# Six of adaLN's scale columns on TensorE from a second weight layout, and h's high part straight from PSUM

## The chip, the cores and the metric

One core of a Trainium2 chip runs the whole program in one launch. The time is the device time of one execution in microseconds (us); three executions of the kernel before were timed. Nothing below is averaged over cores, as there is one.

## What is computed

The reference is a decoder block on x of 512 tokens by 1024 channels, conditioned by one vector c of 1024 numbers. The change lies in its first lines:

```python
mod = jax.nn.silu(c) @ w_ada[l] + b_ada[l]
sh1, sc1, gt1, sh2, sc2, gt2 = jnp.split(mod[:, None, :], 6, axis=-1)
h = rmsnorm(x, norm_pre_mix[l]) * (1.0 + sc1) + sh1
y = token_mixer(h, w_in_mix[l], ...)
```

`mod` is a row of 6144 numbers, a product of one vector with a 1024 by 6144 matrix. The kernel keeps it as 48 columns of 128 (one number to a partition). The first 16 columns, `sh1` (8) and `sc1` (8), must be there before h is, and h is the input of every projection of the token mixer. Behind it stand a gated delta rule, the merge of two branches and an expert retrieval over 16384 rows, in which most of the time goes.

## The kernel before

The program is a row of stages that run one after the other; the change touches the first, `project_stage`. There, x (four tiles of 128 tokens) is squared and summed on ScalarE, scaled by 1/rms on VectorE (xn, L487), transposed in 128x128 blocks on TensorE into PSUM (`turn(k)`, L309; k counts eight blocks of 128 channels), and made into h (channels on partitions, 512 tokens) by one multiply and add with the columns `scale1` and `mod`. TensorE takes float32 products as three products of rounded parts, so every operand is split into a high part (float32r) and the rest: h into `h_hi` and `h_lo`, each weight tile into `w_hi` and `w_lo`.

What sets the order around the change is written out by hand, engine by engine, with semaphores:

- **SP** loads everything in one queue: c spread over partitions, four columns of adaLN's weights (each a 128x1024 tile, transposed, 512 KB, in a ring of eight slots `ada`), the four x tiles, twelve more columns, four projection tiles (`weight_ring`), then two columns and one tile by turns.
- **VectorE** makes each column of `mod` with one pass over a 128x1024 tile (`mod_column`, L475: multiply by silu(c) in PSUM, sum along the row). Per pair of channel blocks it takes four columns (two shifts, two scales) and then four tiny operations on 128x2 (L494, L495, L497, L499): add the bias to the shifts, to the scales, add 1, multiply by the norm's weight. Below, scale2, scale4 and scale6 are the ends of these for blocks 2 and 3, 4 and 5, 6 and 7. It also makes `h_lo` of the last two blocks (L503).
- **ScalarE** makes h twice per block: raw h from PSUM (L424), then its rounding `h_hi` (L427). After block 5 it rounds the first weight tile (`split(0)`, L416), after block 7 the second.
- **GpSimd** makes `h_lo` of blocks 0 to 5 (L385), and then the low part of each weight tile (`rest(n)`, L381).
- **TensorE** turns five blocks, then per block multiplies by the 40 columns of `w_ab` (three matmuls, L337, which end in the decay and beta gates), turns the next, and from block 6 on catches up with the first projection tile: 18 matmuls for blocks 0 to 5 (`project(0, q)`, L320), then blocks 6 and 7. Fifteen more tiles follow.

VectorE's work on the gates (from L507 on) waits for the last `w_ab` matmul, and the convolution of each projection tile (L520, L523) for the tile.

Of the kernel before, what the change touches and what calls it, by code (L numbers as in the profile page):

```python
# [226 lines left out]
def project_stage(nc, a, env):  # L227
# [11 lines left out]
    AR, K2 = 8, 2  # L239
    NB = 5  # L240
    ADA = [m for k in range(0, KT, K2) for m in (*range(SH1 + k, SH1 + k + K2), *range(SC1 + k, SC1 + k + K2))] + list(range(GT1, MOD))
    NA1 = 2 * KT
    N_HERE = N_QKV + N_Z
    with ExitStack() as ctx:
# [14 lines left out]
        dn_w = sb(ctx, "dn_w", [P, 12, 4])  # L259
        exp_a = sb(ctx, "exp_a", [H, 1])  # L260

        s_c, s_const, s_small, s_later, s_wab = (sem(ctx, n) for n in ("c_landed", "const_landed", "small_landed", "later_landed", "wab_landed"))
# [7 lines left out]
             "cols_turned", "gates_exped", "p_last"))  # L270
        V = Steps(sem(ctx, "p_vector"), ["eps"] + [f"{x}0" for x in ("shift", "scale_b", "scale_p", "scale")] + ["rstd"] + [f"xn{t}" for t in range(TT)]
                  + [f"{x}{k}" for k in range(K2, KT, K2) for x in ("shift", "scale_b", "scale_p", "scale")]
                  + ["a_bias", "a_max", "a_neg", "a_min", "b_plus", "beta", "softplus", "g", "G", "G_left", "cols", "be_g"])
        A = Steps(sem(ctx, "p_scalar"), ["c_silu"] + [f"sq{t}" for t in range(TT)] + ["std"] + [x for k in range(KT) for x in (f"h{k}", f"hi{k}")])
        E = Steps(sem(ctx, "p_tensor"), [f"xT{k}" for k in range(KT)])

        xT_ps, proj_ps, ss_ps, ab_ps = bank[0:NB], (bank[3], *bank[0:3]), bank[4], bank[5]
        spread_ps = (bank[5], bank[4])

        with nc.Block() as block:  # L280
            @block.sync
            def _(sp):
                def ada_load(n):
                    if n >= AR:
                        sp.wait_ge(ada_used, n - AR + 1)
                    sp.dma_start(ada[:, n % AR], a["w_ada"][ADA[n]]).then_inc(s_ada[n % AR], 16)

                sp.dma_start(c_in[:], a["c_row"]).then_inc(s_c, 16)
                for n in range(2 * K2):
# [3 lines left out]
                for n in range(2 * K2, NA1):  # L293
                    ada_load(n)
                for n in range(WRING):
# [80 lines left out]
            def _(pool):  # L376
# [6 lines left out]
                for k in range(KT - K2):  # L383
                    pool.wait_ge(*A.after(f"hi{k}"))
                    nc.gpsimd.tensor_tensor(h_lo[:, k, :], h_raw[:, k % 2], h_hi[:, k, :].bitcast(F32), ALU.subtract).then_inc(h_low, 1)  # L385
                for n in range(N_HERE + 2):
                    rest(n)

            @block.scalar
            def _(act):  # L390
                act.dma_start(w_ab[:], a["w_ab"]).then_inc(s_wab, 16)
                act.dma_start(g["cst"][:], a["wide"]).then_inc(s_const, 16)
# [75 lines left out]
            def _(dve):  # L468
# [8 lines left out]

                dve.wait_ge(*A.after("c_silu"))
                for k in range(0, KT, K2):
                    for n in range(2 * k, 2 * k + 2 * K2):  # L480
                        mod_column(n)
                        if n == 5:
                            dve.wait_ge(*A.after("std"))
                            nc.vector.reciprocal(stat[:, 2, :], stat[:, 1, :]).then_inc(*V.step("rstd"))
                            dve.wait_ge(*V.after("rstd"))
                            for t in range(TT):
                                nc.vector.tensor_scalar(xn[:, t * D:(t + 1) * D], x_tok[:, t, :], stat[:, 2, t:t + 1], None, ALU.mult).then_inc(*V.step(f"xn{t}"))  # L487
                    if k == 0:
                        dve.wait_ge(s_small, 16 * 3)
                    if k == K2:  # L490
                        dve.wait_ge(s_later, 16 * 6)
                    dve.wait_ge(ada_used, 2 * k + 2 * K2)
                    sh, sc = slice(SH1 + k, SH1 + k + K2), slice(SC1 + k, SC1 + k + K2)
                    nc.vector.tensor_tensor(mod[:, sh], mod[:, sh], b_ada[:, sh], ALU.add).then_inc(*V.step(f"shift{k}"))  # L494
                    nc.vector.tensor_tensor(mod[:, sc], mod[:, sc], b_ada[:, sc], ALU.add).then_inc(*V.step(f"scale_b{k}"))  # L495
# [35 lines left out]
                for n in range(N_QKV):  # L531
# [25 lines left out]
                assert n_ada + 8 == MOD  # L557
                for m in range(8):
# [7 lines left out]
                dve.wait_ge(ada_used, MOD)  # L566
                nc.vector.tensor_tensor(mod[:, GT1:MOD], mod[:, GT1:MOD], b_ada[:, GT1:MOD], ALU.add).then_inc(last_v, 1)
# [1582 lines left out]
def lay_out(inputs):  # L2150
# [3 lines left out]
    def cols(w, c0, n):  # L2154
# [58 lines left out]
```

## Time and profile before

| | us |
|---|---|
| median of three runs | 1857.72 (1857.22 to 1857.79) |
| profiled execution, first to last instruction | 1856.8 |
| TensorE busy | 1768.2 (95%) |
| VectorE busy | 1307.3 (70%) |
| ScalarE busy | 742.8 (40%) |
| GpSimd busy | 764.5 (41%) |

The span of the profiled execution is 0.9 us under the median of the runs, which hold what lies before the first and after the last instruction too; no separate time of the profiled execution is given. In 40 slices of 46 us each, TensorE is at 0.8 or more of a slice everywhere but in the first (0.3) and one in the middle (0.7), and VectorE at 0.5, 0.9, 0.9 and 0.3 in the first four. The DMA engines are at 0.9 in the first slice and 0.0 to 0.6 in the next ten. TensorE's granted clock is 0.981 of full speed over the span.

### The profile page before, as it was taken

Reading aid. Unit: us, or ns where it says so; the run is one execution under the profiler, and the core shown is the slowest. Engines: PE = TensorE matmul, PEld = TensorE weight load, DVE = VectorE, ACT = ScalarE, POOL = GpSimd, SP = SyncE. Lnnn points to the kernel's source line nnn. Section 1 sums busy time; section 2 is a strip of 40 time slices with the busy share of each in tenths; the row PEclk is TensorE's granted clock in tenths of the full one; section 3 lists DMA queues with packets and bytes.
Section 4 is the critical chain, followed back from the end, with each engine's and each line's share of the span. In section 5 each row is a group of like instructions: output and inputs, shape, how many; then the busy total and the mean of one; then the engine's idle time right before and its main releaser. Section 6 shows DMA issues by size and latency. Waiting matters only on the chain. (4 is left out here: it accounts for less than half of the span.)

```text
span 1856.8 us, 31058 instructions
## 1 busy us (share of the span) xinstructions
PE 1768.2 (95%) x11485; PEld 1564.7 (84%) x11485; DVE 1307.3 (70%) x2777; ACT 742.8 (40%) x1227; POOL 764.5 (41%) x449
## 2 busy tenths in 40 slices
PE   3999999999998989999999999879999999999998
PEld 2666888878877889999999999879998888888887
DVE  5993454553224679878869999756787888777777
ACT  4332332242234233333337767633333333333334
POOL 2333232344442448777753333122454443332330
PEclk9998999999999999999999999989999999999999
DMA  9661101022322249888868999978899999889883
GB/s 356 217 233 71 36 16 34 25 91 91 102 79 103 91 141 314 282 292 292 286 235 281 341 311 331 319 264 285 287 317 337 370 370 359 326 320 328 316 325 145
DMA packets 179267, 432.64 MB, mean 233 GB/s; under 512 B 15816, under 2 KB 91720, under 8 KB 179040
## 3 DMA queue, kind: packets, MB, share of 16 engines
q1 hardware_dynamic: 125088, 273.71, 42.5%
q0 software_dynamic: 36864, 134.23, 20.3%
q10 hardware_dynamic: 17216, 23.36, 3.4%
q8 instruction: 63, 1.03, 0.2%
q14 instruction: 36, 0.29, 0.0%
HBM read 383.54 MB, written 47.71 MB: 232 GB/s over the span
## 5 line engine op out<-in xcount | busy, mean ns | idle before, releaser
L201 POOL DMA_INDIRECT own_rows<-in_peer_v_dram,own_row x128 | 212.3, 1659 | 330.8 <-DVE y_own L2094 312.7
L1988 PE MATMUL banks<-v_hi,coef_lo 128*128 128x512 f32 x756 | 294.6, 390 | 0.0
L1988 PE MATMUL banks<-v_lo,coef_hi 128*128 128x512 f32 x756 | 294.5, 390 | 0.0
L1988 PE MATMUL banks<-v_hi,coef_hi 128*128 128x512 f32 x756 | 294.1, 389 | 0.1
L201 POOL DMA_INDIRECT own_rows<-in_u_rows_dram,own_row x128 | 160.6, 1255 | 233.1 <-DVE own_rows L1733 178.8
L2079 DVE TENSOR_TENSOR v_lo<-weight_ring,v_hi 128x1024 fp32r<-128x1024 f32 x128 | 156.5, 1222 | 24.7 <-ACT v_hi L2027 22.7
L1988 PEld LDWEIGHTS banks<-v_hi,coef_hi 128*128 128x128 f32 x756 | 142.0, 188 | 29.5 <-issue 0.5
L1988 PEld LDWEIGHTS banks<-v_hi,coef_lo 128*128 128x128 f32 x756 | 141.9, 188 | 29.5
L1988 PEld LDWEIGHTS banks<-v_lo,coef_hi 128*128 128x128 f32 x756 | 141.9, 188 | 28.9
L2094 DVE SCALAR_TENSOR_TENSOR y_own<-own_rows,own_coef,y_own 128x1024 f32<-128x1024 f32 x128 | 163.8, 1279 | 1.9 <-DVE y_own L2094 0.5
L1397 PE MATMUL banks<-h_hi,wring_hi 128*128 128x384 f32 (+2 forms) x448 | 155.2, 347 | 4.0 <-ACT gelu_early L1479 2.9
L2027 ACT ACTIVATE v_hi<-weight_ring 128x1024 fp32r<-128x1024 f32 x128 | 135.1, 1055 | 59.4 <-PE banks L1988 48.1
L1527 POOL TENSOR_TENSOR wring_lo<-weight_ring,wring_hi 128x1024 fp32r<-128x1024 f32 x54 | 129.6, 2399 | 65.4 <-ACT wring_hi L1469 65.3
L1397 PE MATMUL banks<-h_lo,wring_hi 128*128 128x384 f32 (+2 forms) x448 | 154.0, 344 | 0.0
L1397 PE MATMUL banks<-h_hi,wring_lo 128*128 128x384 f32 (+2 forms) x448 | 153.9, 344 | 0.0
L2031 ACT ACTIVATE coef_hi<-coef 128x384 fp32r<-128x384 f32 x128 | 67.0, 524 | 211.6 <-DVE coef L2117 211.6
L1469 ACT ACTIVATE wring_hi<-weight_ring 128x1024 fp32r<-128x1024 f32 x54 | 57.3, 1061 | 158.4 <-PE banks L1397 157.9
L1665 DVE SCALAR_TENSOR_TENSOR own_rows<-own_rows,banks 128x1024 f32<-128x1024 f32 x64 | 77.8, 1215 | 52.3 <-DMA own_rows<-in_u_rows_dram,own_row 52.3
L2079 DVE TENSOR_TENSOR coef_lo<-coef,coef_hi 128x384 fp32r<-128x384 f32 x128 | 71.3, 557 | 57.5 <-ACT coef_hi L2031 57.5
L2117 DVE TENSOR_TENSOR coef<-gelu,gate_tiles 128x384 f32<-128x384 f32 x128 | 70.8, 553 | 45.8 <-ACT gelu L2041 45.8
L1165 POOL TENSOR_TENSOR wring_lo<-weight_ring,wring_hi 128x1024 fp32r<-128x1024 f32 x26 | 64.1, 2465 | 88.7 <-ACT wring_hi L1185 88.7
L1787 PE MATMUL banks<-query_hot 128*128 128x128 f32 x768 | 93.6, 278 | 6.7 <-ACT gate_block L1834 5.0
(393 smaller groups left out, 4346.1 us busy)
## 6 DMA issues: line engine op xcount, KB each, us to landing
weight_ring<-in_peer_v_dram SPq DMA_DIRECT2D x128, 512.0 KB, 5.4
weight_ring<-in_peer_u_dram SPq DMA_DIRECT2D x68, 512.0 KB, 4.5
ada<-in_w_ada_dram SPq DMA_DIRECT2D x48, 512.0 KB, 5.7
gate_scratch<-gate_block SPq DMA_DIRECT2D x48, 512.0 KB, 7.0
gate_tiles<-gate_scratch SPq DMA_DIRECT2D x32, 768.0 KB, 6.9
gelu_scratch<-gelu_early ACTq DMA_DIRECT2D x104, 192.0 KB
gelu<-gelu_scratch SPq DMA_DIRECT2D x104, 192.0 KB, 5.6
u_early<-in_peer_u_dram SPq DMA_DIRECT2D x36, 512.0 KB, 7.1
```

Of the source, the lines that this page charges most:

```text
L201: pool.indirect_dma_start(own_rows[:, n % R], None, tables[n // NS], bass.IndirectOffsetOnAxis(ap=own_row[:, n % NS:n % NS + 1], axis=0)). ...
L1165: nc.gpsimd.tensor_tensor(w_lo[:, b % 2], wring[:, b], w_hi[:, b % 2].bitcast(F32), ALU.subtract).then_inc(lo_ready, 1)
L1397: last = nc.tensor.matmul(out, ww[n % HR][:, k, :], x[:, k, t0:nt], start=(k == 0 and m == 0), stop=(k == KT - 1 and m == 2))
L1527: nc.gpsimd.tensor_tensor(w_lo[n % HR][:], w[:, n % WR], w_hi[n % HR][:].bitcast(F32), ALU.subtract).then_inc(lo_ready, 1)
L1665: nc.vector.scalar_tensor_tensor(rows[:, i % R], rows[:, i % R], 1.0, h_psum[:], ALU.mult, ALU.mult, accum_out=own_act[:, bass.ds(n, 1)]). ...
L1787: last = nc.tensor.matmul(bank[2 * (u % 2) + t // 4][:, t % 4 * P:(t % 4 + 1) * P], hot1[:, u % RH, t, :], hot2[:, u % RH, t, :], start=Tr ...
L1988: last = nc.tensor.matmul(y_bank(t, half)[:], w[:, j, t * P:(t + 1) * P], x[:, j, c], start=(first and n == 0), stop=False)
L2027: nc.scalar.activation(v_hi[:, e % G], vt[:, e % G], ACT.Copy).then_inc(v_hi_ready, 1)
L2031: nc.scalar.activation(c_hi[:, e % G], coef[:, e % 2], ACT.Copy).then_inc(c_hi_ready, 1)
L2079: return nc.vector.tensor_tensor(dst, src, hi.bitcast(F32), ALU.subtract)
L2094: nc.vector.scalar_tensor_tensor(y_own[:], rows[:, n % R], own_coef[:, n - NS:n - NS + 1], y_own[:], ALU.mult, ALU.add).then_inc(row_used, 1)
L2117: nc.vector.tensor_tensor(by_block(coef[:, p % 2]), by_block(gel[:, j]), gt[:, i % 2, :, j, :], ALU.mult).then_inc(coef_ready, 1)
```

## The change

- A second layout of the weights, `w_ada_k`, holds the scale columns of blocks 2 to 7 with the contraction on the partitions (512 KB each, as before, now in `qkvT`'s space, which is free until the first convolution). TensorE makes each with eight float32 matmuls of 128x128 weights and one moving column, silu(c) as a column (`c_col`, 128x8, a new small load and a new activation), into bank 3.
- VectorE makes 10 columns ahead of the projections in place of 16; the scale's bias is added straight from PSUM (L520 in the new file).
- ScalarE makes `h_hi` from PSUM in one pass. VectorE makes raw h from PSUM (`raw(k)`, three buffers `h_raw`), for `h_lo` alone.
- Four blocks are turned ahead in place of five, since bank 3 is taken; the first projection tile, whose bank is 3 too, waits for the last use of it (`scale_b6`).
- `split(0)` moves up behind block 3 on ScalarE, and `rest(0)` on GpSimd behind block 3's `h_lo`.

```diff
-    NB = 5
-    ADA = [m for k in range(0, KT, K2) for m in (*range(SH1 + k, SH1 + k + K2), *range(SC1 + k, SC1 + k + K2))] + list(range(GT1, MOD))
-    NA1 = 2 * KT
+    NB = 4
+    ADA = [SH1, SH1 + 1, SC1, SC1 + 1] + list(range(SH1 + K2, SH1 + KT)) + list(range(GT1, MOD))
+    NA1 = KT + K2
...
+                for q in range(0, NPE, K2):
+                    for n in range(2 * K2 + q, 2 * K2 + q + K2):
+                        ada_load(n)
+                    for n in range(q, q + K2):
+                        sp.dma_start(ada_k[:, n], a["w_ada_k"][n]).then_inc(s_adak[n], 16)
+                    if q == K2:
+                        sp.dma_start(wring[:, 0], a["w_proj"][0]).then_inc(s_w[0], 16)
...
+                def ada_columns(q0):
+                    for q in range(q0, q0 + K2):
+                        pe.wait_ge(s_adak[q], 16)
+                        for k in range(KT):
+                            last = nc.tensor.matmul(ada_ps[:, q:q + 1], ada_k[:, q, k, :], c_col[:, k:k + 1], start=(k == 0), stop=(k == KT - 1))
+                        last.then_inc(ada_col, 1)
+
+                pe.wait_ge(c_col_ready, 1)
+                ada_columns(0)
                 pe.wait_ge(s_const, 16)
                 pe.wait_ge(*V.after(f"xn{TT - 1}"))
                 for k in range(NB):
                     turn(k)
+                pe.wait_ge(*V.after("scale_b2"))
+                ada_columns(K2)
...
+                            pe.wait_ge(*V.after("scale_b6"))
                             pe.wait_ge(lo_ready, 1)
...
                     if k + NB < KT:
+                        pe.wait_ge(*A.after(f"hi{k}"))
+                        pe.wait_ge(*V.after(f"raw{k}"))
                         turn(k + NB)
+                    if k == 1:
+                        pe.wait_ge(*V.after("scale_b4"))
+                        ada_columns(2 * K2)
...
-                    nc.scalar.activation(h_raw[:, k % 2], xT_ps[k % NB][:], ACT.Identity, bias=mod[:, SH1 + k:SH1 + k + 1],
-                                         scale=scale1[:, k:k + 1]).then_inc(*A.step(f"h{k}"))
-                    act.wait_ge(*A.after(f"h{k}"))
-                    nc.scalar.activation(h_hi[:, k, :], h_raw[:, k % 2], ACT.Copy).then_inc(*A.step(f"hi{k}"))
-                    if k == KT - 3:
+                    nc.scalar.activation(h_hi[:, k, :], xT_ps[k % NB][:], ACT.Identity, bias=mod[:, SH1 + k:SH1 + k + 1],
+                                         scale=scale1[:, k:k + 1]).then_inc(*A.step(f"hi{k}"))
+                    if k == 3:
                         split(0)
...
+                    src = ada_ps[:, k - K2:k] if by_pe else mod[:, sc]
+                    nc.vector.tensor_tensor(mod[:, sc], src, b_ada[:, sc], ALU.add).then_inc(*V.step(f"scale_b{k}"))
...
+                def raw(k):
+
+                    dve.wait_ge(*A.after(f"hi{k}"))
...
+                    if HRAW <= k < KT - K2 + HRAW:
+                        dve.wait_ge(h_low, k - HRAW + 1)
+                    nc.vector.tensor_scalar(h_raw[:, k % HRAW], xT_ps[k % NB][:], scale1[:, k:k + 1], mod[:, SH1 + k:SH1 + k + 1],
+                                            ALU.mult, ALU.add).then_inc(*V.step(f"raw{k}"))
```

On SP, the loads behind the x tiles (`w_ada` is the old layout, `w_ada_k` the new). Before:

```order
L292 DMA x_tok<-in_x_dram 128x1024 x4
L286 DMA ada<-in_w_ada_dram 128x1024 x4
L286 DMA ada<-in_w_ada_dram 128x1024 [waits ada_used] x8
L296 DMA weight_ring<-in_w_proj_dram 128x1024 x4
L286 DMA ada<-in_w_ada_dram 128x1024 [waits ada_used] x2
```

Now:

```order
L301 DMA x_tok<-in_x_dram 128x1024 x4
L295 DMA ada<-in_w_ada_dram 128x1024 x2
L306 DMA qkvT<-in_w_ada_k_dram 128x1024 x2
L295 DMA ada<-in_w_ada_dram 128x1024 x2
L306 DMA qkvT<-in_w_ada_k_dram 128x1024 x2
L308 DMA weight_ring<-in_w_proj_dram 128x1024
L295 DMA ada<-in_w_ada_dram 128x1024 [waits ada_used] x2
L306 DMA qkvT<-in_w_ada_k_dram 128x1024 x2
L310 DMA weight_ring<-in_w_proj_dram 128x1024 x3
```

The same 16 loads stand in another order, with the first projection tile (L308) five places ahead of the last pair of columns.

On TensorE, the start of the program. Before:

```order
L309 MATMUL banks<-cst,xn 128x128 [waits p_vector,const_landed]
L309 MATMUL banks<-cst,xn 128x128 x19
L337 MATMUL banks<-h_hi,wab_parts 40x512 [waits h_low_ready,ab_lo_ready]
L337 MATMUL banks<-h_lo,wab_parts 40x512
L337 MATMUL banks<-h_hi,wab_parts 40x512
L309 MATMUL banks<-cst,xn 128x128 x4
```

Now (the pair L330 on `ada_k_landed4` and `5` comes behind two more blocks, in the same form):

```order
L330 MATMUL banks<-c_col,qkvT 128x1 [waits ada_k_landed0,c_col_silu]
L330 MATMUL banks<-c_col,qkvT 128x1 x7
L330 MATMUL banks<-c_col,qkvT 128x1 [waits ada_k_landed1]
L330 MATMUL banks<-c_col,qkvT 128x1 x7
L323 MATMUL banks<-cst,xn 128x128 [waits p_vector,const_landed]
L323 MATMUL banks<-cst,xn 128x128 x15
L330 MATMUL banks<-c_col,qkvT 128x1 [waits ada_k_landed2,p_vector]
L330 MATMUL banks<-c_col,qkvT 128x1 x7
L330 MATMUL banks<-c_col,qkvT 128x1 [waits ada_k_landed3]
L330 MATMUL banks<-c_col,qkvT 128x1 x7
L363 MATMUL banks<-h_hi,wab_parts 40x512 [waits h_low_ready,ab_lo_ready]
```

Forty-eight matmuls on one column stand in the queue ahead of, between and behind the turns.

On VectorE, from the end of xn to block 3. Before (L494 to L499 are the four tiny operations):

```order
L475 SCALAR_TENSOR_TENSOR ada,mod<-ada,banks 128x1024 [waits ada_landed6]
L475 SCALAR_TENSOR_TENSOR ada,mod<-ada,banks 128x1024 [waits ada_landed7]
L494 TENSOR_TENSOR mod<-mod,b_ada 128x2 [waits ada_used,later_landed]
L495 TENSOR_TENSOR mod<-mod,b_ada 128x2
L497 TENSOR_SCALAR scale<-mod 128x2 [waits p_vector]
L499 TENSOR_TENSOR scale<-scale,norms 128x2 [waits p_vector]
L475 SCALAR_TENSOR_TENSOR ada,mod<-ada,banks 128x1024 [waits ada_landed0]
```

Now (four lines of the tiny operations for blocks 2 and 3 come first, then):

```order
L508 SCALAR_TENSOR_TENSOR ada,mod<-ada,banks 128x1024 [waits ada_landed6]
L508 SCALAR_TENSOR_TENSOR ada,mod<-ada,banks 128x1024 [waits ada_landed7]
L533 TENSOR_SCALAR h_raw<-banks,scale,mod 128x512 [waits p_vector,p_scalar]
L533 TENSOR_SCALAR h_raw<-banks,scale,mod 128x512 [waits p_scalar]
L516 TENSOR_TENSOR mod<-mod,b_ada 128x2 [waits ada_used]
L520 TENSOR_TENSOR mod<-banks,b_ada 128x2 [waits ada_column_done]
L522 TENSOR_SCALAR scale<-mod 128x2 [waits p_vector]
L524 TENSOR_TENSOR scale<-scale,norms 128x2 [waits p_vector]
L533 TENSOR_SCALAR h_raw<-banks,scale,mod 128x512 [waits p_vector,p_scalar]
L533 TENSOR_SCALAR h_raw<-banks,scale,mod 128x512 [waits h_low_ready,p_scalar]
```

The tiny operations of a pair now wait for TensorE (`ada_column_done`), and the passes that make raw h stand between the column passes in VectorE's queue.

## Rows read from the trace of the kernel before

**Rows 1.** The page's first line.
```profile
span 1856.8 us, 31058 instructions
```
**Rows 2.** Stretches of 5 us: length, busy us (instructions) by engine, PEclk, DMA share, GB/s.
```profile
core 0: us, PE busy (x) PEld busy (x) DVE busy (x) ACT busy (x) POOL busy (x), PEclk, DMA share, GB/s
...
35.00:40.00 5.00, 2.71 (x6) 0.66 (x6) 4.97 (x9) 2.89 (x5) 4.20 (x3) 0.74 1.03 410
40.00:45.00 5.00, 4.26 (x12) 3.37 (x12) 2.56 (x7) 3.66 (x5) 0.69 (x1) 0.57 0.78 257
45.00:50.00 5.00, 5.00 (x23) 3.67 (x22) 0.00 (x0) 1.12 (x2) 2.39 (x1) 1.00 0.57 176
50.00:55.00 5.00, 5.00 (x23) 4.11 (x23) 4.84 (x6) 3.13 (x5) 2.39 (x1) 1.00 0.86 325
```
**Rows 3.** Timeline, 22 to 41 us: start, duration, engine, line, operation.
```profile
22.54 2.74 DVE L487 TENSOR_SCALAR xn<-x_tok,stat 128x1024 f32<-128x1024 f32 x4
...
25.42 4.50 PE L309 MATMUL banks<-cst,xn 128*128 128x128 f32 x20 [25.42 <-DVE xn L487]
...
30.84 0.60 PE L309 MATMUL banks<-cst,xn 128*128 128x128 f32 x4
...
31.08 2.63 POOL L385 TENSOR_TENSOR h_lo<-scT,h_hi 128x512 fp32r<-128x512 f32 x2 [0.34 <-ACT h_hi L427]
...
32.89 0.84 DVE L494 TENSOR_TENSOR mod<-mod,b_ada 128x2 f32<-128x2 f32 x1
...
34.03 0.16 DVE L499 TENSOR_TENSOR scale<-scale,norms 128x2 f32<-128x2 f32 x1
...
38.33 2.35 POOL L381 TENSOR_TENSOR wring_lo<-weight_ring,wring_hi 128x1024 fp32r<-128x1024 f32 x1
...
38.79 1.91 DVE L494 TENSOR_TENSOR mod<-mod,b_ada 128x2 f32<-128x2 f32 x1
...
40.74 0.80 PE L320 MATMUL banks<-h_hi,wring_hi 128*128 128x512 f32 x1 [0.81 <-POOL wring_lo L381]
```
**Rows 4.** Timeline: the matmul behind the first 18 of tile 0, and VectorE's next work.
```profile
47.27 0.40 PE L337 MATMUL banks<-h_hi,wab_parts 128*40 128x512 f32 x1
...
50.06 0.74 DVE L507 TENSOR_SCALAR xn<-banks,dt_bias 8x512 f32<-8x512 f32 x1 [5.29 <-PE banks L337]
```
**Rows 5.** Single loads: the fifth column, the first projection tile; issue and landing.
```profile
L286 SPq DMA_DIRECT2D ada<-in_w_ada_dram x1: 443/443/443, 5.8 to 5.8; - x1
...
DMA to landing us min/median/max: 14.1/14.1/14.1
...
L296 SPq DMA_DIRECT2D weight_ring<-in_w_proj_dram x1: 432/432/432, 28.0 to 28.0; - x1
...
DMA to landing us min/median/max: 7.3/7.3/7.3
```
**Rows 6.** Groups by line, 0 to 165 us: passes from PSUM to SBUF.
```profile
L520 DVE TENSOR_SCALAR xn<-banks,dn_w 128x512 f32<-128x512 f32 x12 | 8.7, 728 | 2.7 <-PE banks L320 2.7
...
L424 ACT ACTIVATE scT<-banks,mod,scale 128x512 f32<-128x512 f32 x8 | 6.2, 770 | 10.6 <-PE banks L309 5.2 <-DVE scale L499 5.1 <-POOL h_lo L385 0.2
```
**Rows 7.** Small matmuls: weight loads with eight moving columns; float32 matmuls of a line.
```profile
L370 PEld LDWEIGHTS banks<-cst,decay_rows x12: 133/137/138, 93.9 to 94.6; 8*128 8x128 f32 x12
...
L364 PE MATMUL banks<-scT,cst 128*16 128x512 f32 x16 | 8.9, 637 | 4.3 <-ACT scT L440 4.3
```
**Rows 8.** Timeline, the delta stage: VectorE between two GpSimd operations.
```profile
186.06 0.76 POOL L736 TENSOR_TENSOR AT<-LT,cst 128x256 f32<-128x256 f32 x1
186.19 1.17 DVE L924 SCALAR_TENSOR_TENSOR qgT<-qkv_tile,egT 128x512 f32<-128x512 f32 x1
186.76 1.20 POOL L737 TENSOR_TENSOR CT<-LT,cst 128x256 f32<-128x256 f32 x1
```
**Rows 9.** Stretches of 0.2 us of line L771 (matmuls of 8 rows): PE, PEld, PEclk.
```profile
172.40:172.60 0.20, 0.20 (x4) 0.20 (x4) 1.00 0.00 0
...
173.40:173.60 0.20, 0.20 (x4) 0.20 (x4) 1.00 0.00 0
...
174.00:174.20 0.20, 0.00 (x0) 0.00 (x0) 0.50 0.00 0
```

More of the change, by code:

```diff
@@ L260, in project_stage @@
         exp_a = sb(ctx, "exp_a", [H, 1])
+        c_col = sb(ctx, "c_col", [P, KT])
+        ada_k = qkvT[:].rearrange("p (q n) t -> p q (n t)", q=NPE).rearrange("p q (k m) -> p q k m", k=KT)
+        ada_ps = bank[3]
+        s_ck, c_col_ready, ada_col = sem(ctx, "c_col_landed"), sem(ctx, "c_col_silu"), sem(ctx, "ada_column_done")
+        s_adak = [sem(ctx, f"ada_k_landed{q}") for q in range(NPE)]
         s_c, s_const, s_small, s_later, s_wab = (sem(ctx, n) for n in ("c_landed", "const_landed", "small_landed", "later_landed", "wab_landed"))
@@ L292, in _ @@
                     sp.dma_start(x_tok[:, t, :], a["x"][t * P:(t + 1) * P, :]).then_inc(s_x[t], 16)
-                for n in range(2 * K2, NA1):
-                    ada_load(n)
-                for n in range(WRING):
+                for q in range(0, NPE, K2):
[5 more added lines that the diff above has]
+                        sp.dma_start(wring[:, 0], a["w_proj"][0]).then_inc(s_w[0], 16)
+                for n in range(1, WRING):
                     sp.dma_start(wring[:, n], a["w_proj"][n]).then_inc(s_w[n], 16)
@@ L384, in _ @@
                     pool.wait_ge(*A.after(f"hi{k}"))
-                    nc.gpsimd.tensor_tensor(h_lo[:, k, :], h_raw[:, k % 2], h_hi[:, k, :].bitcast(F32), ALU.subtract).then_inc(h_low, 1)
-                for n in range(N_HERE + 2):
+                    pool.wait_ge(*V.after(f"raw{k}"))
+                    nc.gpsimd.tensor_tensor(h_lo[:, k, :], h_raw[:, k % HRAW], h_hi[:, k, :].bitcast(F32), ALU.subtract).then_inc(h_low, 1)
+                    if k == 3:
+                        rest(0)
+                for n in range(1, N_HERE + 2):
                     rest(n)
@@ L390, in _ @@
             def _(act):
+                act.dma_start(c_col[:], a["c_col"]).then_inc(s_ck, 16)
                 act.dma_start(w_ab[:], a["w_ab"]).then_inc(s_wab, 16)
@@ L401, in _ @@
                 last.then_inc(*A.step("c_silu"))
+                act.wait_ge(s_ck, 16)
+                nc.scalar.activation(c_col[:], c_col[:], ACT.Silu).then_inc(c_col_ready, 1)
                 for dst, name in small[3:]:
@@ L476, in mod_column, with scales @@
                                                    accum_out=mod[:, m:m + 1]).then_inc(ada_used, 1)
[L478 to L492, printed above, removed]
+                def scales(k):
                     sh, sc = slice(SH1 + k, SH1 + k + K2), slice(SC1 + k, SC1 + k + K2)
+                    by_pe = k >= K2
+                    dve.wait_ge(ada_used, 2 * K2 + k if by_pe else 2 * K2)
                     nc.vector.tensor_tensor(mod[:, sh], mod[:, sh], b_ada[:, sh], ALU.add).then_inc(*V.step(f"shift{k}"))
-                    nc.vector.tensor_tensor(mod[:, sc], mod[:, sc], b_ada[:, sc], ALU.add).then_inc(*V.step(f"scale_b{k}"))
+                    if by_pe:
+                        dve.wait_ge(ada_col, k)
+                    src = ada_ps[:, k - K2:k] if by_pe else mod[:, sc]
+                    nc.vector.tensor_tensor(mod[:, sc], src, b_ada[:, sc], ALU.add).then_inc(*V.step(f"scale_b{k}"))
                     dve.wait_ge(*V.after(f"scale_b{k}"))
@@ L499, in _ @@
                     nc.vector.tensor_tensor(scale1[:, k:k + K2], scale1[:, k:k + K2], norms[:, 0, k:k + K2], ALU.mult).then_inc(*V.step(f"scale{k}"))
+                def raw(k):
+                    dve.wait_ge(*A.after(f"hi{k}"))
+                    if k % K2 == 0:
+                        dve.wait_ge(*V.after(f"scale{k}"))
+                    if HRAW <= k < KT - K2 + HRAW:
+                        dve.wait_ge(h_low, k - HRAW + 1)
+                    nc.vector.tensor_scalar(h_raw[:, k % HRAW], xT_ps[k % NB][:], scale1[:, k:k + 1], mod[:, SH1 + k:SH1 + k + 1],
+                                            ALU.mult, ALU.add).then_inc(*V.step(f"raw{k}"))
@@ new lines, in low @@
+                def low(k):
+                    dve.wait_ge(*A.after(f"hi{k}"))
+                    dve.wait_ge(*V.after(f"raw{k}"))
+                    nc.vector.tensor_tensor(h_lo[:, k, :], h_raw[:, k % HRAW], h_hi[:, k, :].bitcast(F32), ALU.subtract).then_inc(h_low_end, 1)
+                dve.wait_ge(*A.after("c_silu"))
+                for n in range(2 * K2):
+                    mod_column(n)
+                dve.wait_ge(s_small, 16 * 3)
+                scales(0)
+                for n in range(2 * K2, 3 * K2):
+                    mod_column(n)
@@ new lines, in _ @@
+                dve.wait_ge(*A.after("std"))
+                nc.vector.reciprocal(stat[:, 2, :], stat[:, 1, :]).then_inc(*V.step("rstd"))
+                dve.wait_ge(*V.after("rstd"))
+                for t in range(TT):
+                    nc.vector.tensor_scalar(xn[:, t * D:(t + 1) * D], x_tok[:, t, :], stat[:, 2, t:t + 1], None, ALU.mult).then_inc(*V.step(f"xn{t}"))
+                dve.wait_ge(s_later, 16 * 6)
+                scales(2)
+                for n in range(3 * K2, 4 * K2):
+                    mod_column(n)
@@ L501, in _ @@
+                raw(0)
+                raw(1)
+                scales(4)
+                raw(2)
+                raw(3)
+                for n in range(4 * K2, NA1):
+                    mod_column(n)
+                raw(4)
+                raw(5)
+                scales(6)
                 for k in range(KT - K2, KT):
-                    dve.wait_ge(*A.after(f"hi{k}"))
-                    nc.vector.tensor_tensor(h_lo[:, k, :], h_raw[:, k % 2], h_hi[:, k, :].bitcast(F32), ALU.subtract).then_inc(h_low_end, 1)
+                    raw(k)
@@ L504, in _ @@
+                for k in range(KT - K2, KT):
+                    low(k)
                 nc.vector.tensor_scalar(neg_sel[:], sel_head[:, :, 0:1].rearrange("h n o -> h (n o)"), -1.0, None, ALU.mult)
@@ L2171, in lay_out @@
         "c_row": np.broadcast_to(f["c"], (P, D)),
+        "c_col": f["c"][0].reshape(KT, P).T,
+        "w_ada_k": cols(f["w_ada"][0], (SC1 + 2) * P, KT - 2),
         "w_ada": f["w_ada"][0].T.reshape(MOD, P, D),
```

21 lines of the change are left out of this document (12 added, 9 removed).

## The prediction

> **What bounds the kernel now.** The span is 1856.8 us [rows 1]; the change touches its first 50. I read the stretches of 5 us first. VectorE is busy 4.97 of 5 us up to 40 us, then falls to 2.56 and to nothing, while TensorE rises to 5.00 of 5; from 50 on VectorE is full again [rows 2]. So adaLN's columns on VectorE lead up to the first projection tile, and the tile leads to VectorE's gate work at 50.06, which waited 5.29 us for TensorE [rows 4]. Whatever moves that 50.06 moves everything behind it: VectorE is loaded from there on, then the stages follow one another. A shift of it by d is thus a shift of the total by d.
>
> The timeline then shows what the tile waits for. Its first matmul starts at 40.74, released by GpSimd's rest of the weight tile (38.33 to 40.68); 18 matmuls bring it to 47.27 [rows 3, 4], at first slowly: the granted clock is 0.74 and 0.57 around 40 us, and 1.00 after [rows 2], that is, TensorE was for a time at 1.2 GHz and not at 2.4. GpSimd's rest waited in turn for scale4, done at 34.19 (L499) [rows 3], through ScalarE's blocks 4 and 5.
>
> **Loads.** The 16 loads are the same bytes in another order. The fifth column landed at 5.8 + 14.1 = 19.9, the first projection tile at 28.0 + 7.3 = 35.3 [rows 5]; twelve loads lie between, 1.28 us each, one behind the other. In the new order the columns for TensorE, k0 to k5, come at 22.5, 23.7, 27.6, 28.9, 34.0 and 35.3, columns 6 and 7 for VectorE at 25.0 and 26.3, and the projection tile at 30.1. The last of adaLN thus lands when the projection tile did, not sooner. The small `c_col` load costs at most a few tenths; I take nothing, since VectorE waits for x and columns there.
>
> **A column on TensorE.** One float32 matmul of the code is two instructions in the trace (L364: 8 in the code, 16 in the row [rows 7]), so a column is 16 and a pair 32 weight loads with a matmul of one moving column. The nearest row is L370, with 8 moving columns, at 2.4 GHz: 12 starts from 93.9 to 94.6, 0.064 us apart [rows 7]; so 2.05 us a pair. At 1.2 GHz I double it: 4.1 us. As bounds I keep these two.
>
> The Trainium skill (TensorE: Matmul & The Clock Gate, LDWEIGHTS (loading the stationary operand)) gives a weight load of 128 columns as columns over 1.2, so an estimate of 107 ns whatever the clock. By it a pair would cost 3.4 us; the row's 64 ns between starts speaks against it, and the sum would rise by 0.2 us in the quick case below.
>
> **The turns.** Before, 20 transposes took 4.50 us from 25.42, 0.225 each, and later four took 0.60 [rows 3]: TensorE began at 1.2 GHz (the first pace is near twice the second, although no clock record stands there). Now k0 and k1 come first in its queue, on an engine that has done nothing: 22.5 plus 2.05, then 2.05 more, ends at 26.6. So the turns start 1.2 us later than at 25.42; 16 of them end at 30.2. Behind them k2 and k3 end at 32.3 at 2.4 GHz, or at 34.3.
>
> **VectorE.** xn ends at 25.3 [rows 3]; scale2 then waits for k1 and ends near 27.4. Two columns at 1.15 (four of them lie between 34.19 and 38.79 [rows 3]) and two `raw` passes at 0.73 (L520, from PSUM, same shape [rows 6]) bring it to 31.2. Six columns less (6.9 us) against eight raw passes more (5.8 us): VectorE is hardly relieved. Now come the tiny operations of blocks 4 and 5, and here GpSimd matters. While GpSimd works, VectorE's operations with SBUF inputs stand still: L494 took 0.84 beside `h_lo` and 1.91 beside the weight rest, each to GpSimd's end, where L499 takes 0.16 [rows 3]. If both queue, VectorE gets in at the border of two GpSimd operations: its 1.17 us operation waited for the first, and the second, issued at 186.76, stretched to 1.20 where its like took 0.76 [rows 8]. So the shift's bias waits for block 0's `h_lo` (31.95), and "add 1" for block 1's (33.4): scale4 at 33.7, or 34.9 if k3 is late. Before: 34.19. The step that should have come sooner does not.
>
> **GpSimd.** With scale4 at 33.7, raw 2 ends at 34.5 and GpSimd starts block 2: two `h_lo` (2.63), the weight rest (2.35), two more `h_lo` (2.63) and 0.3 for VectorE's operations between: 42.4 (43.6 in the late case). All these durations are in [rows 3]. VectorE meanwhile has raw 2 and 3, two columns, raw 4 and 5 (5.2 us): 38.7, in time. Before, the weight rest came last and the tile started at its end, 40.68; now blocks 4 and 5 come last, as `w_ab`'s matmuls of all six stand in TensorE's queue ahead of tile 0. Scale6, with "add 1" and the norm's weight each behind one `h_lo`, ends at 43.6; its blocks 6 and 7 are two ScalarE passes at 0.77 [rows 6], two raw and two low parts later, near 47, about when 18 matmuls are through.
>
> **TensorE up to tile 0.** At 2.4 GHz: 42.4 plus three matmuls of 0.22 (23 in 5.00 us [rows 2]) is a start at 43.1. Its own queue is the other bound. From 30.2 to tile 0 it has 64 instructions of columns, 18 of `w_ab` and 16 turns: at 1.2 GHz 64 x 0.128, 18 x 0.44 and 16 x 0.225, or 8.2 + 7.9 + 3.6 us, a start at 49.9. If the clock rises near 37 us, the queue is through by 43 and GpSimd's late 43.6 decides: a start at 44.3.
>
> **The sum.** The 18 matmuls take 18 x 0.22 = 4.0 us at 2.4 GHz, or 6.5 as before (47.27 less 40.74). Against 47.27: start 43.1 gives 47.1 or 49.6 (-0.2 or +2.3 us), start 44.3 gives 48.3 or 50.8 (+1.0 or +3.5). Nothing tells the four apart well enough, and I take their mean, +1.7 us. Nothing is owed behind tile 0: the same 32 columns, 16 tiles and convolutions follow, in the same order, and the ScalarE passes saved are hidden under VectorE. So the span becomes 1858.5; the median, 0.92 us above the span before, goes from 1857.72 to **1859.4**. That is under 0.2% (3.7 us), about what a measurement of this kernel can tell from no change.
>
> **Rivals.**
>
> *TensorE stays at 1.2 GHz through the columns* (slower). The clock rose before after transposes back to back and fell after a lull. Now the transposes are fewer, and one-column matmuls stand between. Rows 9 are the warning: matmuls of eight rows kept TensorE busy without a gap from 172.4 to 173.6 at 1.00, and at 174.0 the clock was at 0.50 all the same [rows 9]. Then the start is 49.9, the 18 matmuls 4.0 to 6.5 us, the end 53.9 to 56.4: +6.6 to +9.1 us, or 1864.3 to 1866.8. Between this and the forecast, the clock may rise for a part. It decides as soon as the queue is later than GpSimd's 43.6, that is, if the clock has not risen by about 38 us. Against it: after 34 us `w_ab`'s 512-column matmuls and turns stand close together, which is what went before the rise in the old trace. Chance 0.22.
>
> *The waits on GpSimd fall elsewhere and TensorE is at 2.4 GHz* (faster). Were "add 1" not held, scale4 would end at 32.8, blocks 4 and 5 at 41.2, tile 0 would start at 41.8 and its 18 matmuls end at 45.8: -1.5 us, 1856.2. For it: scale6 is then ready at 39 and no longer behind the tile; a small operation could slip in between. Against it: every tiny operation of the old trace that met GpSimd waited to its end. Chance 0.2. A gain over 3.7 us would need tile 0 to be through at 43.6, that is, to start at 39.6, before GpSimd can have done its 7.6 us behind raw 2; I leave 0.04 for what I don't see.
>
> *The moves cost nothing on either side* is no case of its own: it lies inside the forecast's four corners.
>
> **The numbers.** Forecast (-0.2 to +3.5 us) 0.54, faster rival 0.2, slower rival 0.22, unseen gain 0.04. The range from 1856.0 (the faster rival's end) to 1865.0 (the lower half of the slower one) leaves out some 0.15 to 0.2. The slower rival counts nearly whole as slower by over 0.2%, with a little of the forecast's upper corner; the rest is within.
>
> **What would show it.** In the new profile: k5 lands near 35.3; the first turn starts near 26.6, not 25.4; scale4 ends at 33.5 to 35; "add 1" lasts about 1.2 us beside `h_lo`; the wait ahead of tile 0 names GpSimd's `h_lo` or nothing (TensorE's own queue); tile 0 starts at 43 to 45 and VectorE's gate work at about 51.8. It is wrong if tile 0 starts under 41 (the holds or the clock don't bite), if TensorE is busy with its queue to 48, or if the gate work's shift does not show in the total.

## The result and the profile after

The changed kernel takes **1868.9 us** (median of 6 runs, 1863.64 to 1874.88) against 1857.76 for the kernel before in the same batch (6 runs): ratio 1.0066, 95% interval 1.0054 to 1.0079. It is slower by 11.1 us, 9.5 us over the forecast and 3.9 us past the range. The profiled execution was the slowest of the six (1874.88 us).

The page's first lines after [rows 1], with the busy time of three engines:

```profile
span 1873.1 us, 31260 instructions
...
PE 1789.1 (96%) x11581; PEld 1586.2 (85%) x11581; DVE 1310.0 (70%) x2773; ACT 738.3 (39%) x1220; POOL 765.9 (41%) x449
```

Stretches of 5 us after, with the columns of [rows 2]:

```profile
25.00:30.00 5.00, 5.00 (x25) 5.00 (x25) 0.71 (x5) 0.00 (x0) 0.00 (x0) 1.00 1.03 413
...
35.00:40.00 5.00, 5.00 (x24) 4.76 (x25) 0.26 (x2) 0.00 (x0) 0.78 (x1) 1.00 1.02 408
...
45.00:50.00 5.00, 5.00 (x33) 4.07 (x33) 1.94 (x5) 0.18 (x1) 3.43 (x3) 0.76 0.57 207
```

VectorE, full to 40 us before [rows 2], is busy 0.71 us of the first of these stretches and 0.26 us of the second; TensorE is busy in all of each. The bound has moved. The timeline after, which answers to [rows 3, 4], shows to what:

```profile
22.58 6.96 PE L330 MATMUL banks<-c_col,qkvT 128*128 128x1 f32 x32 [22.58 <-DMA qkvT<-in_w_ada_k_dram]
...
29.40 3.65 PE L323 MATMUL banks<-cst,xn 128*128 128x128 f32 x16
29.57 0.16 DVE L520 TENSOR_TENSOR mod<-banks,b_ada 128x2 f32<-128x2 f32 x1 [4.22 <-PE banks L330]
...
32.84 6.83 PE L330 MATMUL banks<-c_col,qkvT 128*128 128x1 f32 x32
...
33.78 0.80 DVE L516 TENSOR_TENSOR mod<-mod,b_ada 128x2 f32<-128x2 f32 x1
...
39.53 0.63 PE L363 MATMUL banks<-h_hi,wab_parts 128*40 128x512 f32 x1
...
39.71 0.16 DVE L520 TENSOR_TENSOR mod<-banks,b_ada 128x2 f32<-128x2 f32 x1 [5.13 <-PE banks L330]
...
40.10 0.16 DVE L524 TENSOR_TENSOR scale<-scale,norms 128x2 f32<-128x2 f32 x1
...
43.79 3.80 PE L330 MATMUL banks<-c_col,qkvT 128*128 128x1 f32 x32
...
47.82 0.63 DVE L522 TENSOR_SCALAR scale<-mod 128x2 f32<-128x2 f32 x1
...
52.70 0.39 PE L345 MATMUL banks<-h_hi,wring_hi 128*128 128x512 f32 x1
...
59.85 0.74 DVE L575 TENSOR_SCALAR xn<-banks,dt_bias 8x512 f32<-8x512 f32 x1 [3.24 <-PE banks L363]
```

Three pairs of columns (L330, x32) take 6.96, 6.83 and 3.80 us. VectorE waits 4.22 and 5.13 us for the first two. Scale4 ends at 40.26 (34.19 before), tile 0 starts at 52.70 (40.74 before) and the gate work at 59.85 (50.06 before): the front alone, from the start to the gate work, is 9.8 us longer.

PEclk needs care: it reads 1.00 from 25 to 40 us, where a 512-column matmul takes 0.63 us (39.53), as it does at 1.2 GHz, against 0.39 at 52.70. Up to its first clock record the column shows 1.00 for want of one; the pace of a known shape tells the level.

### The profile page after: what moved, and what is told of

The parts are those of the page before. It is cut to its first block and busy times, and to the rows that moved or that the text cites. A ratio compares the mean times of both kernels' runs of the same rounds, so it can differ in the third digit from the quotient of the medians.

```text
span 1873.1 us, 31260 instructions
## 1 busy us (share of the span) xinstructions
PE 1789.1 (96%) x11581; PEld 1586.2 (85%) x11581; DVE 1310.0 (70%) x2773; ACT 738.3 (39%) x1220; POOL 765.9 (41%) x449
```

## The experiments

Gate work (front) is the start of VectorE's first gate operation in the run's profile; the total is the median, with its ratio to the kernel before on the same chip.

| run | gate work, us | total, us | ratio, interval |
|---|---|---|---|
| after | 59.85 | 1868.9 | 1.0066 [1.0054, 1.0079] |
| e1 | 48.27 | 1857.61 | 1.0004 [0.9991, 1.0017] |
| e2 | 56.32 | 1870.84 | 1.0077 [1.0061, 1.0092] |
| e3 | 49.80 | 1858.98 | 1.0011 [0.9997, 1.0026] |
| e4 | 54.94 | 1866.72 | 1.0055 [1.004, 1.007] |
| e5 | 56.55 | 1869.61 | 1.006 [1.004, 1.0079] |
| e6 | 60.15 | 1871.16 | 1.0067 [1.005, 1.0084] |
| e7 | 62.98 | 1873.56 | 1.0083 [1.0065, 1.01] |
| e8 | 53.10 | 1862.58 | 1.0028 [1.0016, 1.0039] |
| e9 | 50.56 | 1865.67 | 1.0046 [1.0031, 1.0062] |
| e10 | 49.35 | 1859.17 | 1.0015 [1.0003, 1.0026] |
| e11 | 52.36 | 1857.52 | 0.9998 [0.9989, 1.0007] |
| e12 | 57.60 | 1862.37 | 1.0032 [1.002, 1.0044] |

**e1: one matmul of eight for each column.**

```diff
-    for k in range(KT):
+    for k in range(1):
```

> The changed kernel with one of the eight matmuls of each scale column on TensorE (k = 0 only), the same loads, waits and order; it leaves out seven eighths of the contraction of six scale columns. Theory (the columns' weight loads fill TensorE's queue, 0.213 us per instruction at 1.2 GHz, 17.6 us in all, in front of the turns and of the w_ab matmuls): a pair falls from 6.9 to about 0.9 us, the first turn comes back from 29.4 to about 25.5 us, scale4 from 40.3 to about 32.5, and VectorE's gate work from 59.9 to 49 to 52 us; the time to 1856 to 1860. Rival A (the loads' new order and the waits between the engines make the loss, whatever a column costs): the gate work stays over 56 us, the time over 1864. Rival B (VectorE's raw passes and GpSimd's hold on VectorE's small operations): about half comes back, gate work at 54 to 55 us.

The whole loss went. Timeline of e1:

```profile
41.12 0.39 PE L345 MATMUL banks<-h_hi,wring_hi 128*128 128x512 f32 x1
...
48.27 0.74 DVE L575 TENSOR_SCALAR xn<-banks,dt_bias 8x512 f32<-8x512 f32 x1 [2.24 <-PE banks L363]
```

Loads, waits and h's new route are all still there, and the gate work starts 1.8 us before [rows 4]. What costs is the number of column instructions on TensorE. It also bounds the change: with an eighth of the column instructions the total is no lower than before.

**e2: columns on TensorE, h by ScalarE's two passes as before.**

```diff
-    nc.scalar.activation(h_hi[:, k, :], xT_ps[k % NB][:], ...)
+    nc.scalar.activation(h_raw[:, k % HRAW], xT_ps[k % NB][:], ...)
+    nc.scalar.activation(h_hi[:, k, :], h_raw[:, k % HRAW], ACT.Copy)
```

> The columns on TensorE as in the change, but h made as before: raw h and then its high part on ScalarE (three buffers), no raw passes on VectorE. Theory (TensorE's queue of columns): hardly anything comes back, gate work at 57 to 60 us, 1866 to 1869. Rival B (raw passes on VectorE and GpSimd's hold): the gate work comes back to 54 or sooner and the time under 1863.

Nothing came back: h's route is not the cause. (That its front is 3.5 us shorter than after's is not the route's doing either: see e5.)

**e3: the kernel before with the first projection tile loaded and split early.**

```diff
-    for n in range(2 * K2, NA1):
+    for n in range(2 * K2, 6 * K2):
         ada_load(n)
+    sp.dma_start(wring[:, 0], a["w_proj"][0]).then_inc(s_w[0], 16)
+    for n in range(6 * K2, NA1):
+        ada_load(n)
...
-    if k == KT - 3:
+    if k == 3:
         split(0)
...
+    if k == 3:
+        rest(0)
```

> The kernel before with one part of the change alone: the first projection tile is loaded ahead of the last four columns, split on ScalarE behind block 3 and on GpSimd behind block 3's low part; all columns on VectorE, h as before. If GpSimd's late weight rest is what starts tile 0 in the kernel before (40.7 us): GpSimd ends block 5 at about 38.7, scale6 is no longer held by the weight rest (39.3 in place of 41.2), tile 0 starts at 39.4 to 40, gate work at 48.5 to 49.5 in place of 50.1, and the time falls by 0.6 to 1.6 us. If a late load of the last columns takes its place: no gain or up to 1.3 us lost.

The front gained 0.26 us, less than expected, and tile 0 started no sooner (41.66, 40.74 before); the total shows no difference. Moving the weight split is worth nothing that can be measured.

**e4: idle matmuls ahead of the first pair.**

```diff
+    for n in range(14):
+        nc.tensor.matmul(ab_ps[:], C["ident"], g["cst"][:, 0:512], ...)
     ada_columns(0)
```

> The changed kernel with 14 idle float32 matmuls of 512 columns on TensorE ahead of the first pair of columns (from about 8 us on, into a bank that is overwritten later), so that TensorE has been busy when the first weights land. Clock theory (at 2.4 GHz a column's instruction takes 0.11 us in place of 0.213): the first pair takes 3.5 to 4 us in place of 7, the first turn starts at 26 to 26.5 us in place of 29.4, the later pairs are as slow as before if the one-column matmuls let the clock fall again; gate work 2 to 4 us sooner, 1865 to 1867. If the clock is not the reason for 0.213: the pair stays at 7 us.

The loss is 8.0 us in its batch, where the changed kernel lost 11.1 and 12.1 (e5) in theirs: some of it came back, as expected, though the intervals overlap. Timeline of e4:

```profile
23.12 3.83 PE L330 MATMUL banks<-c_col,qkvT 128*128 128x1 f32 x32
26.82 3.40 PE L323 MATMUL banks<-cst,xn 128*128 128x128 f32 x16
30.05 3.93 PE L330 MATMUL banks<-c_col,qkvT 128*128 128x1 f32 x32
33.84 0.63 PE L365 MATMUL banks<-h_hi,wab_parts 128*40 128x512 f32 x1
```

The first pair now runs at 2.4 GHz (3.83 us), but the turns behind it are at 1.2 GHz again (3.40 us for 16, 0.21 each), the second pair at 2.4, and what follows it at 1.2 (0.63). Each pair of columns is followed by a fall of the clock.

**e5: the changed kernel once more.** No edit.

> The changed kernel once more, unedited, as the yardstick of this batch. The profile of e2 had its second pair of columns in 3.85 us, the profile of the changed kernel in 6.83 us, though TensorE had done the same work up to there. If the granted clock rises at different points of the same work from execution to execution, this profile may have its gate work anywhere between 55 and 60 us (after: 59.85), and the total lies at 1866 to 1871 us; if old and new route of h set that difference, the gate work starts at 59.5 to 60.2 us again.

```profile
33.06 3.86 PE L330 MATMUL banks<-c_col,qkvT 128*128 128x1 f32 x32
...
56.55 0.74 DVE L575 TENSOR_SCALAR xn<-banks,dt_bias 8x512 f32<-8x512 f32 x1 [3.24 <-PE banks L363]
```

The second pair took 3.86 us here and 6.83 in the first profile of the same kernel: the clock rises at different points of the same work, and in these two profiles the front is 6.5 and 9.8 us over before. e2, at 6.3, is close to e5.

**e6: 8 rows in place of 128.**

```diff
-    ada_k[:, q, k, :], c_col[:, k:k + 1]
+    ada_k[0:8, q, k, :], c_col[0:8, k:k + 1]
```

> Every column contracts over 8 of its 128 rows alone (the rest of the contraction is left out); the number of instructions, the moving columns and the loads stay. The prediction took its price from a row with 8 rows. If the rows set the price, a pair of columns takes 2.0 us at 2.4 GHz and 4.1 us at 1.2 GHz or less, the gate work starts at 51 to 53 us and the total is 1857 to 1862 us. If the price does not hang on the rows, a pair keeps 3.5 to 7 us and the total is 1866 to 1870 us.

**e9: transposes of 8 rows, the form of [rows 7], two for each matmul.**

```diff
-    nc.tensor.matmul(ada_ps[:, q:q + 1], ada_k[:, q, k, :], c_col[:, k:k + 1], ...)
+    nc.tensor.transpose(ada_ps[:, 8 * q:8 * q + 8], ada_k[0:8, q, k // 2, :], ident[0:8, 0:8])
```

> In place of each float32 matmul of a column (two instructions) stand two transposes of 8 rows with 8 moving columns, the very form of the row that the prediction took its price from; the contraction is left out, the loads and the count of instructions stay. If that row's price is right for its own form and wrong for a float32 matmul, a pair takes 4.1 us at 1.2 GHz and 2.05 us at 2.4 GHz, as predicted: turns at 26.6 to 27 us, gate work at 51 to 55 us, total 1858 to 1863 us. If the place sets the price (any weight load costs 0.11 or 0.22 us here), it stays at 1867 to 1871 us.

One row each from the groups by line (busy us, mean ns of one, idle before), 20 to 60 us, of after, e6 and e9: three pairs, 96 instructions.

```profile
L330 PE MATMUL banks<-c_col,qkvT 128*128 128x1 f32 x96 | 17.6, 317 | 22.6 <-DMA qkvT<-in_w_ada_k_dram 22.6
```
```profile
L330 PE MATMUL banks<-c_col,qkvT 8*128 8x1 f32 x96 | 17.9, 316 | 22.3 <-DMA qkvT<-in_w_ada_k_dram 22.3
```
```profile
L330 PE MATMUL banks<-cst,qkvT 8*128 8x8 f32 x96 | 9.4, 235 | 22.5 <-DMA qkvT<-in_w_ada_k_dram 22.5
```

The rows don't matter (17.6, 17.9), the form does (9.4). Timeline of e9:

```profile
22.50 3.55 PE L330 MATMUL banks<-cst,qkvT 8*128 8x8 f32 x32 [22.50 <-DMA qkvT<-in_w_ada_k_dram]
25.98 3.67 PE L323 MATMUL banks<-cst,xn 128*128 128x128 f32 x16
...
37.51 2.25 PE L330 MATMUL banks<-cst,qkvT 8*128 8x8 f32 x32
...
43.38 0.40 PE L345 MATMUL banks<-h_hi,wring_hi 128*128 128x512 f32 x1
...
50.56 0.74 DVE L575 TENSOR_SCALAR xn<-banks,dt_bias 8x512 f32<-8x512 f32 x1 [2.73 <-PE banks L363]
```

A transpose of 8 rows costs 3.55/32 = 0.11 us at 1.2 GHz and 2.25/32 = 0.07 at 2.4, near the prediction's 0.128 and 0.064; an instruction of a float32 matmul costs 6.96/32 = 0.22 and 3.80/32 = 0.12 (all with the tail of the last one). With the cheap form the forecast's front appears (tile 0 at 43.4, gate work 0.5 us late), but the total does not: 1865.67, above the 1858 to 1863 expected.

**e7: the turns ahead of the first pair.**

```diff
-    ada_columns(0)
     for k in range(NB):
         turn(k)
+    ada_columns(0)
     ada_columns(K2)
```

> The first four turns go ahead of the first pair of columns on TensorE. Theory (the columns' weight loads fill TensorE, wherever they stand): the turns start at 25.3 us instead of 29.4 us, the columns come after them, TensorE stands still from 22.6 to 25.3 us, and what that costs is given back by a clock that the turns raise earlier: 1865 to 1871 us. Rival (the first turn held up behind the columns is what is paid): the 4 us come back, 1863 to 1865 us, with the gate work at 55 to 56 us.

```profile
25.19 3.65 PE L323 MATMUL banks<-cst,xn 128*128 128x128 f32 x16 [25.19 <-DVE mod L516]
28.64 6.82 PE L330 MATMUL banks<-c_col,qkvT 128*128 128x1 f32 x32
35.71 6.99 PE L330 MATMUL banks<-c_col,qkvT 128*128 128x1 f32 x32 [0.25 <-DVE mod L520]
```

1873.56, worse than both theories had it: the four turns (25.19 to 28.64) did not raise the clock, and both pairs behind them ran at 1.2 GHz (6.82 and 6.99 us). The gate work came 3.1 us later than in the profile after, somewhat more than TensorE's idle time from 22.6 to 25.2; the 4 us of the late turn are no cost of their own.

**e8: 64 equal moving columns in place of one.**

```diff
-    matmul(ada_ps[:, q:q + 1], ada_k[:, q, k, :], c_col[:, k:k + 1], ...)
+    matmul(ada_ps[:, 64 * q:64 * q + 64], ada_k[:, q, k, :], c_col[:, k:k + 1].broadcast_to([P, 64]), ...)
```

> Each matmul of a column moves 64 equal columns instead of one, into 64 columns of the bank, of which one is read; instructions and weight loads stay. If the clock falls back because a one-column matmul leaves the array idle, it now rises during the first pair and stays: the later pairs take 3.5 us each, the gate work starts at 53 to 56 us, the total is 1861 to 1865 us. If the moved columns do not bear on the clock, nothing comes back: 1867 to 1872 us.

7.0 us less than the changed kernel in the same batch (e5), for 63 useless columns per matmul; in the two profiles the front is 3.45 us shorter (53.10 against 56.55), and the rest lies behind it. Timeline of e8:

```profile
22.59 7.06 PE L330 MATMUL banks<-c_col,qkvT 128*128 128x64 f32 x32 [22.59 <-DMA qkvT<-in_w_ada_k_dram]
...
32.70 3.68 PE L330 MATMUL banks<-c_col,qkvT 128*128 128x64 f32 x32
36.20 0.42 PE L363 MATMUL banks<-h_hi,wab_parts 128*40 128x512 f32 x1
...
38.48 3.68 PE L330 MATMUL banks<-c_col,qkvT 128*128 128x64 f32 x32
41.98 0.42 PE L363 MATMUL banks<-h_hi,wab_parts 128*40 128x512 f32 x1
```

At 2.4 GHz a pair costs the same with 64 columns (3.68) as with one (3.80 to 3.93), and the matmuls behind each pair stay at 0.42 us: the clock does not fall. But the first pair took 7.06 us, 1.2 GHz to its end: the wider matmuls kept the clock up and did not raise it, which the expectation had asked of them too. So the loss has two parts, the price of an instruction and a clock that fell behind one-column matmuls.

**e10: e8 with 13 idle matmuls ahead.**

```diff
+    for n in range(13):
+        nc.tensor.matmul(ab_ps[:], C["ident"], g["cst"][:, 0:512], ...)
```

> e8 with 13 idle float32 matmuls of 512 columns ahead of the first pair, so that the first pair too runs at 2.4 GHz. If the loss is made of the price per weight load and the clock and of nothing else, three pairs at 3.5 us remain, the first turn starts at 26 to 27 us, the gate work at 49 to 51 us, and the total is 1857 to 1860 us, no difference to the kernel before. If another wait stands behind it, the total stays at 1861 us or above.

```profile
23.07 3.68 PE L330 MATMUL banks<-c_col,qkvT 128*128 128x64 f32 x32
26.59 1.92 PE L323 MATMUL banks<-cst,xn 128*128 128x128 f32 x16
28.34 3.68 PE L330 MATMUL banks<-c_col,qkvT 128*128 128x64 f32 x32
...
49.35 0.74 DVE L577 TENSOR_SCALAR xn<-banks,dt_bias 8x512 f32<-8x512 f32 x1 [2.09 <-PE banks L365]
```

The three pairs, the turns and the gate work's matmuls are at 2.4 GHz, the gate work starts 0.7 us earlier than before, and the total is 2.4 us above (ratio 1.0015). The price is the full one here and the clock is high; in e9 the price is the low one and the first two pairs are at 1.2 GHz. Each brings the front back to within 0.7 us of before, so the front's loss takes both, the price and the low clock. No version here beats the kernel before.

**e11 and e12: the kernel before, its front delayed.** n idle matmuls (1, 8) behind the last one that the gate work waits for.

```diff
+    for n in range(8):
+        last = nc.tensor.matmul(ss_ps[:], C["ident"], g["cst"][:, 0:512], ...)
     last.then_inc(ab_done, 1)
```

> The kernel before with one idle float32 matmul of 512 columns (two instructions, 0.88 us at 2.4 GHz) behind the last matmul that the gate work waits for: the front ends 0.9 us later and nothing else changes. This tests the prediction's sentence that a shift of the front is a shift of the total. By it the total rises by 0.9 us, within what can be told from no change (ratio under 1.002). If the later stages' clock hangs on when the front ends, as e9 suggests (front 0.5 us later in its profile, total 9 us), the total rises by 5 to 9 us.

> The same with eight idle matmuls, 7.0 us: the front of e5 (gate work 6.5 us later than before) without any column on TensorE. If a shift of the front is a shift of the total: 1864 to 1865 us, ratio near 1.0038. If the later stages add to it as in e5 and e2: 1868 to 1871 us, ratio 1.006 to 1.0075.

A gate work 2.3 us later (0.9 was expected) costs nothing measurable, one 7.5 us later 4.9 us; yet e5, with 6.5 us, lost 12.1, and e9, with 0.5, lost 8.9 (medians, against 1857.54 and 1856.78). Where each profile parts from the profile before is seen at two starts that every profile has, VectorE's first instruction in the delta stage and in the stage behind it. Differences to the profile before, in us:

| profile | gate work (50.06) | delta stage (161.96) | stage behind it (376.51) | span (1856.8) |
|---|---|---|---|---|
| after | +9.8 | +10.2 | +11.7 | +16.3 |
| e5 | +6.5 | +6.8 | +11.9 | +12.8 |
| e9 | +0.5 | +0.8 | +6.0 | +6.6 |
| e7 | +12.9 | +13.3 | +13.1 | +13.3 |
| e12 | +7.5 | +4.8 | +4.0 | +4.2 |

One profile each; executions of one kernel differ by some us themselves (before: 1854.18 to 1859.42 in the first batch), so the table tells where the time went, not how often. In e7 the front's delay is the span's. In e5 and e9 the delta stage adds 5.1 and 5.2 us, in the profile after 1.5, and there 4.6 more come behind it. In e12 2.7 us go between the gate work and the delta stage. The delta stage, columns as in [rows 2], before, after, e5, e9, e7, e12:

```profile
161.96:376.51 214.55, 203.38 (x3432) 175.77 (x3433) 100.39 (x206) 65.01 (x137) 64.41 (x50) 0.96 0.10 32
```
```profile
172.16:388.19 216.03, 204.97 (x3433) 176.92 (x3433) 100.44 (x206) 65.00 (x137) 64.37 (x50) 0.95 0.10 31
```
```profile
168.71:388.38 219.67, 208.60 (x3433) 179.61 (x3433) 100.37 (x206) 65.00 (x137) 64.37 (x50) 0.93 0.09 31
```
```profile
162.75:382.48 219.73, 208.75 (x3432) 179.73 (x3433) 100.34 (x205) 65.06 (x137) 64.36 (x50) 0.93 0.09 31
```
```profile
175.30:389.62 214.32, 203.34 (x3433) 175.68 (x3433) 100.53 (x206) 65.02 (x137) 64.42 (x50) 0.96 0.10 32
```
```profile
166.79:380.48 213.69, 202.55 (x3432) 175.08 (x3433) 100.37 (x205) 65.07 (x137) 64.41 (x50) 0.96 0.10 32
```

The other engines' busy time is the same to 0.2 us. TensorE's, and the length, go with the granted clock: 0.93 in e5 and e9 (and e2), 0.95 in after and e6, 0.96 in before, e7, e12, e1, e3, e4, e8, e10 and e11. Two profiles of one kernel, after and e5, differ by 3.6 us here. What decides the clock in that stage is open; a later front alone does not lower it, by e7, e11 and e12.

## Why the prediction was wrong

- **The loads were right.** The last column for TensorE, whose rows after (issue, landing) are these, landed at 19.8 + 15.5 = 35.3, as forecast, and nothing waited for it. (The first projection tile stands three places ahead of the last pair of columns, not five; the landings were worked out with the right place.)

```profile
L306 SPq DMA_DIRECT2D qkvT<-in_w_ada_k_dram x1: 1076/1076/1076, 19.8 to 19.8; - x1
...
DMA to landing us min/median/max: 15.5/15.5/15.5
```

- **"A column on TensorE" is the step that failed first.** It took 0.064 us an instruction from L370 [rows 7] and doubled it for 1.2 GHz. That row is of transposes. e9 shows its price to hold for transposes (0.07 and 0.11), e6 that rows don't make the difference, and in the change an instruction of a float32 matmul costs 0.12 and 0.22. So a pair is 3.8 or 6.9 us, not 2.05 or 4.1. Front with the one form 50.56, with the other 59.85 (56.55 in e5): 6 to 9.3 us. The row was chosen by its few columns and not by its operation. The better row was at hand: L771, the line of [rows 9], is a float32 matmul with 8 rows and 128 moving columns; sixteen of its instructions in the kernel before, at 2.4 GHz, took 2.05/16 = 0.13 us each, twice the price taken. At 2.4 GHz the true price would have done little harm (e10); at 1.2 GHz it is what made the loss.

```profile
171.91 2.05 PE L771 MATMUL banks<-decay_rows,small 8*128 8x128 f32 x16
```

- **The page I set aside was right where the clock is 2.4 GHz.** The Trainium skill (TensorE: Matmul & The Clock Gate, LDWEIGHTS (loading the stationary operand)) gave an estimate of 107 ns, a pair of 3.4 us; e8 and e10 measure 3.68 with the last one's tail. It also says that the columns of a weight load count, not its rows, and e6 agrees (17.9 us against 17.6). At 1.2 GHz the instruction took twice that, so "whatever the clock", as the prediction read it, does not hold; the transposes of e9 took 0.11 at 1.2 GHz, which is the figure, and 0.07 at 2.4, which is under it. The 0.2 us by which the sum was to rise with that figure has no term in the sum: with 3.4 us a pair the prediction's own times have k3 done at 32.9, ahead of the 33.4 that decides.
- **The clock: the slower rival came true, to which the prediction gave 0.22.** In the profile after, TensorE was busy without a gap and stayed at 1.2 GHz up to the third pair; in e5 it was at 2.4 GHz for the second and third pair and fell behind each. e8 shows on this kernel what keeps the clock: the same instructions with 64 moving columns did not let it fall. What raises it sooner or later is open. The rival's time (1864.3 to 1866.8) was short, as it rested on the same price: its columns behind the turns were 64 x 0.128 = 8.2 us, and 6.83 + 3.80 = 10.6 came, after a first pair of 6.96 for 4.1. And the range ended at 1865.0, inside the rival's own time.
- **VectorE and GpSimd.** The holds are there (L516 0.80 and L522 0.63 us beside GpSimd), but scale4 waited for TensorE alone and ended at 40.26, not 33.7 to 34.9. Ahead of tile 0 TensorE's own queue decided, the second of the two bounds that the text named. (The prediction's 38.7 for VectorE's raw 5 is 33.7 + 5.2 = 38.9; nothing hangs on it.)
- **"A shift of it by d is thus a shift of the total by d" fell too.** Of the profiles in the table it holds in e7 alone. The stages behind the front do not keep their length: the delta stage takes 213.7 to 219.7 us in the profiles shown. Of the 11.1 us (a median), 6.5 to 9.8 stand in the front by two profiles of the changed kernel; the rest lies behind it, with a lower clock in the delta stage for a part, and why it is lower is not settled.

## What to carry to other kernels

Price an instruction from a row of the same operation and type, not of the same shape: here a float32 matmul with a 128-column weight load took about twice as long as a transpose, and one moving column saved nothing over 64. Before moving a matrix-vector product to TensorE, count its weight loads and ask what keeps the clock up while they run. And a front that looks 1 us better or worse should be timed before it is credited, since a later stage with the same work took 3.6 us more in one profile of the same kernel than in the other.

## What was not expected of the hardware

- Float32 matmuls back to back for 7 us left TensorE at 1.2 GHz, with one moving column (after, e5, e7) and with 64 (e8). After 3.8 us of one-column ones at 2.4 GHz the clock fell (e4); with 64 columns it stayed up (e8, e10).
- The granted clock rose at different points of identical work: the second pair took 6.83 and 3.86 us in two profiles of one kernel.
- The delta stage, 100 us behind the front and with the same instructions, ran at a mean clock of 0.93 to 0.96 and took 213.7 to 219.7 us in the profiles shown; two profiles of one kernel differ by 3.6 us.
